# Opening of a hybrid decoder layer: x scaled row by row ahead of plain transposes, both halves of u read from PSUM, the first weight tile's pieces set between the x tiles

## The reference

```python
def rmsnorm(x, w):
    xf = x.astype(jnp.float32)
    y = xf * lax.rsqrt(jnp.mean(xf * xf, axis=-1, keepdims=True) + EPS)
    return (y * w.astype(jnp.float32)).astype(x.dtype)

    u = rmsnorm(h, norm_w)                       # h: meta tokens, then x; 1040 rows of 1024
    proj = jnp.einsum('btd,dc->btc', u, w_in)    # w_in: 1024 x 4104
    cuts = np.cumsum([HG_WIDTH, HG_WIDTH, HG_WIDTH, HG_WIDTH, 3 * GDN_WIDTH, GDN_WIDTH, GDN_HEADS])
    hg_q, hg_f, hg_i, hg_z, gd_qkv, gd_z, gd_a, gd_b = jnp.split(proj, [int(c) for c in cuts], axis=-1)
    ...
    g = -jnp.exp(gdn_A_log.astype(f32)) * jax.nn.softplus(gd_a.astype(f32) + gdn_dt_bias.astype(f32))
```

## Time and profile before

| | us |
|---|---|
| median of 3 runs | 728.11 |
| lowest, highest | 727.39, 728.21 |
| the profiled execution | 727.87 |
| its span in the trace | 726.2 |
| PE busy | 706.3 (97%) |
| DVE, ACT, POOL busy | 436.0, 304.3, 351.9 |

### The profile page before, as it was taken

How to read it: one execution, slowest core, us unless ns; L and a number is a source line. 1 busy time by engine, 2 the same in 40 slices (tenths; PEclk the granted TensorE clock), 3 DMA queues, 4 the chain that set the end, 5 groups by cost and what they waited for, 6 DMA issues and landing times. The chain is left out here.

```text
span 726.2 us, 13528 instructions
## 1 busy us (share of the span) xinstructions
PE 706.3 (97%) x4858; PEld 678.3 (93%) x4858; DVE 436.0 (60%) x1018; ACT 304.3 (42%) x800; POOL 351.9 (48%) x471
## 2 busy tenths in 40 slices
PE   7999999999999999999999999999999999999995
PEld 7799999999999999999999999999999998888884
DVE  6845356279882472598934634989436257776257
ACT  6644431635544315445444154445442352232333
POOL 5782332257562422376714232767342557756333
PEclk9999999999999999999999999999999999999999
DMA  8355332221213317450639141202244306221004
GB/s 265 35 65 84 29 34 57 50 29 31 36 33 61 53 42 64 21 39 17 40 51 71 40 69 25 35 9 48 51 67 152 86 32 209 68 64 52 30 36 195
DMA packets 63989, 44.93 MB, mean 62 GB/s; under 512 B 17438, under 2 KB 59044, under 8 KB 63924
## 3 DMA queue, kind: packets, MB, share of 16 engines
q1 hardware_dynamic: 63924, 44.07, 33.7%
HBM read 35.82 MB, written 7.65 MB: 60 GB/s over the span
## 5 line engine op out<-in xcount | busy, mean ns | idle before, releaser
L258 PE MATMUL proj<-uTh,w_high 128*128 128x352 f32 (+4 forms) x768 | 261.6, 341 | 2.4 <-PEq L1742 2.4
L258 PE MATMUL proj<-uTh,w_low 128*128 128x352 f32 (+4 forms) x768 | 246.0, 320 | 0.0
L258 PE MATMUL proj<-uTl,w_high 128*128 128x352 f32 (+4 forms) x768 | 245.5, 320 | 0.0
L258 PEld LDWEIGHTS proj<-uTh,w_high 128*128 128x128 f32 x768 | 145.3, 189 | 3.3 <-issue 3.1
L258 PEld LDWEIGHTS proj<-uTl,w_high 128*128 128x128 f32 x768 | 145.3, 189 | 0.0
L258 PEld LDWEIGHTS proj<-uTh,w_low 128*128 128x128 f32 x768 | 144.4, 188 | 0.0
L276 POOL TENSOR_TENSOR w_low<-w_raw,w_high 128x256 fp32r<-128x256 f32 (+1 forms) x54 | 71.7, 1328 | 84.0 <-ACT w_high L268 36.6
L1242 POOL TENSOR_TENSOR f_suffix<-f_suffix,f_prefix 128x192 f32<-128x192 f32 x84 | 55.5, 661 | 27.7 <-DVE f_prefix L1458 21.2
L1662 PEld LDWEIGHTS mix<-level_x 128*128 128x128 f32 x448 | 60.7, 191 | 3.4 <-issue 1.2
L1662 PE MATMUL mix<-level_x 128*128 128x64 f32 x448 | 59.8, 266 | 0.0
L1505 DVE SCALAR_TENSOR_TENSOR conv_out<-conv_in,hg_taps,conv_out 128x352 f32<-128x352 f32 (+2 forms) x81 | 51.7, 638 | 0.5
(11 more groups left out here) (308 smaller groups left out, 1397.0 us busy)
## 6 DMA issues: line engine op xcount, KB each, us to landing
w_raw<-in_w_in SPq DMA_DIRECT2D x32, 512.0 KB, 8.3
x_tile<-in_x SPq DMA_DIRECT2D x8, 512.0 KB, 6.7
w_raw<-y_scratch SPq DMA_DIRECT2D x8, 384.0 KB, 4.4
decay<-gamma_scratch SPq DMA_DIRECT2D x4, 576.0 KB, 3.7
landing<-in_w_out SPq DMA_DIRECT2D x4, 512.0 KB, 8.0
landing<-in_x SPq DMA_DIRECT2D x3, 512.0 KB, 6.4
out_y<-landing SPq DMA_DIRECT2D x3, 512.0 KB, 2.6
y_scratch<-gd_y SPq DMA_DIRECT2D x6, 192.0 KB, 1.8
```

Of the source, the lines that this page charges most:

```text
L258: last = pe.matmul(acc[:, 0:tw], w[j % 2][:, k, :], u[:, k, t0:t0 + tw], start=(k == 0 and i == 0), stop=(k == KT - 1 and i == 2))
```

## The change

- The norm weight is loaded as one row spread over 128 partitions (`nrow`, 512 KB in SBUF), between the first and the second x tile. It is no longer among the small parameter rows.
- DVE multiplies x in place by the inverse root and that row (`scale_tile`, 128x1024) before PE turns it.
- PE turns the scaled tile with plain transposes against the identity. The diagonal matrices, their ring and the copy of the identity in PSUM are gone.
- ACT rounds straight from PSUM, DVE subtracts straight from PSUM and frees the bank. POOL has no part in the low halves any more, and `u_part` is gone.
- ACT squares three tiles ahead instead of four.
- The first weight tile is loaded after x tile 5, ahead of the gate columns and of x tiles 6 to 8. ACT casts it after tile 2's halves, POOL makes its low part, in four quarters, after the inverse root of tile 5.
- On PE, parts 0 to 7 of the first piece and the first gate piece stand between the transposes of tiles 4 to 8. After tile 8 come the second piece, two gate pieces and the third piece; the gate rows are turned after the third piece and the cumulative gate is made after the fifth.
- The transpose of the parameter rows stands after tile 3. The clearing of the masks on DVE stands after the x tiles.

```diff
+            sp.dma_start(nrow[:, :], norm_w[0:1, :].broadcast_to([P, D])).then_inc(nrow_in, 16)
+            load_x(2)
+            load_x(3)
             sp.wait_ge(cleared, 1)
...
-            for i in range(2, XS):
-                load_x(i)
+            load_x(4)
+            load_x(5)
+            load_tile(0, tile_cols("gd", GD_KINDS[0], 0))
             sp.dma_start(gate_raw[:, :, :], w_in_v[:, :, AB_COLS:AB_COLS + 2 * HEADS]).then_inc(gate_in, 16)
+            load_x(6)
+            load_x(7)
...
+            for i in range(NC):
                 rstd_tile(i)
-            for i in range(NC):
-                low_part(pool, 2 * i + 1)
-                if i + AHEAD < NC:
-                    rstd_tile(i + AHEAD)
-            early_low(0)
+                if i == 5:
+                    pool.wait_ge(w_high, 1)
+                    for part in range(LOW_PARTS):
+                        ks = slice(part * KT // LOW_PARTS, (part + 1) * KT // LOW_PARTS)
+                        last = pool.tensor_tensor(wl[0][:, ks, :], raw[1][:, ks, :], wh[0][:, ks, :].bitcast(F32), ALU.subtract)
+                    last.then_inc(w_low, 1)
...
+            def scale_tile(i):
...
+                dve.scalar_tensor_tensor(out=x_, in0=x_, scalar=rstd[0:w, i:i + 1], in1=nrow[0:w, :],
+                                         op0=ALU.mult, op1=ALU.mult).then_inc(scaled, 1)
+
+            def low_part(i, half):
+
+                dve.wait_ge(u_high, 2 * i + half + 1)
+                dve.tensor_tensor(u_of(ul, i, half), turned(i, half), u_of(uh, i, half).bitcast(F32), ALU.subtract
+                                  ).then_inc(bank_free(front, ("x", i, half)), 1)
...
+                        last = pe.transpose(ap[:, k * P:k * P + w], xt[i % XS][0:w, c0:c0 + P], ident[0:w, 0:w])
                     last.then_inc(done, 1)
-            for g in range(len(PIECES)):
+                if i == EARLY - 1:
+                    pe.wait_ge(rows_in, 64)
+                    ap, done = take(pe, front, "rows")
+                    pe.transpose(ap[:, 0:P], rows[:, :], ident[:, :]).then_inc(done, 1)
+                if i in (EARLY, EARLY + 1):
+                    project(range(3 * (i - EARLY), 3 * (i - EARLY) + 3))
+                if i == EARLY + 2:
+                    project(range(6, PARTS))
+                    gate_piece(0, range(2))
+                if i == EARLY + 3:
+                    gate_piece(0, range(2, KT))
+            project(range(PARTS, 2 * PARTS))
+            for g in range(1, len(PIECES)):
                 gate_piece(g)
-            project(range(0, PARTS))
+            project(range(2 * PARTS, 3 * PARTS))
             pe.wait_ge(gate_out, len(PIECES))
```

More of the change, by code:

```diff
@@ L343, in hybrid_layer @@
     XS = 8
-    DIAGS = 3
     xt = [sb(f"x_tile{i}", [P, D], F32, s1) for i in range(XS)]
-    ut = [sb(f"u_part{i}", [P, 512], F32, s1) for i in range(3)]
-    diag = [sb(f"rstd_diag{i}", [P, P], F32, s1) for i in range(DIAGS)]
+    nrow = sb("norm_row", [P, D], F32, s1)
     square = sb("square", [P, D], F32, s1)
@@ L365, in hybrid_layer @@
     pmask = sb("pad_mask", [P, 1], F32, s1)
-    front = Bank(["rows"] + [("x", i, half) for i in range(NC) for half in range(2)]
-                 + [("ab", g) for g in range(NG)] + ["gam", "tot", "gam_rows"], 4)
+    EARLY = 4
+    front = Bank([("x", i, half) for i in range(EARLY) for half in range(2)] + ["rows"]
+                 + [("x", i, half) for i in range(EARLY, NC) for half in range(2)] + [("ab", g) for g in range(NG)] + ["gam", "tot", "gam_rows"], 4)
     gbank = bank[4:6]
-    ident_ps = bank[5][:, 384:384 + P]
-    AHEAD = 4
+    AHEAD = 3
     with nc.Block() as block:
@@ L519, in _, with high_part @@
         def _(act):
-            def high_part(n):
-                i, half = divmod(n, 2)
-                w = rows_of(i)
-                t0 = 0 if i == 0 else META + (i - 1) * P
-                freed(act, front, ("x", i, half))
-                act.copy(uh[:, 4 * half:4 * half + 4, t0:t0 + w],
-                         ut[n % 3][:, 0:4 * w].rearrange("p (k t) -> p k t", k=4)).then_inc(u_high, 1)
+            def high_part(i, half):
+                full(act, front, ("x", i, half))
+                act.copy(u_of(uh, i, half), turned(i, half)).then_inc(u_high, 1)
             def square_tile(i):
@@ L562, in _ @@
             for i in range(NC):
[L563 to L566 removed]
                 for half in range(2):
[L568 removed]
+                    high_part(i, half)
                 if i + AHEAD < NC:
                     square_tile(i + AHEAD)
+                if i == 2:
+                    early_high(0)
                 if i == 4:
@@ L661, in _ @@
             dve.memset(ab_t[:, 0:PAD], 0.0)
+            dve.wait_ge(nrow_in, 16)
+            scale_tile(0)
+            for i in range(NC):
+                if i + 1 < NC:
+                    scale_tile(i + 1)
+                for half in range(2):
+                    low_part(i, half)
+                if i == EARLY:
+                    lower_bounds()
+                if i == 5:
+                    dve.wait_ge(gate_high, 1)
+                    dve.tensor_tensor(gate_l, gate_raw[:, :, :], gate_h.bitcast(F32), ALU.subtract).then_inc(gate_low, 1)
             dve.memset(mwork[:, :, :], 0.0).then_inc(mask_set, 1)
@@ L760, in project, with u_ready, gate_piece @@
                     if part == 0 and j == 0:
-                        for low in u_low:
-                            pe.wait_ge(low, 1 + -(-(t0 + tw - META) // P))
+                        u_ready(t0 + tw)
                     project_part(pe, n, "front", 1)
-            def gate_piece(g):
+            def u_ready(t1):
+                for half in range(2):
+                    freed(pe, front, ("x", -(-(t1 - META) // P), half))
+            def gate_piece(g, ks=range(KT)):
                 t0, tw = PIECES[g]
-                for low in u_low:
-                    pe.wait_ge(low, 1 + -(-(t0 + tw - META) // P))
-                pe.wait_ge(gate_low, 1)
-                if g >= 2:
-                    pe.wait_ge(gate_out, g - 1)
-                for k in range(KT):
+                if ks[0] == 0:
+                    u_ready(t0 + tw)
+                    pe.wait_ge(gate_low, 1)
+                    if g >= 2:
+                        pe.wait_ge(gate_out, g - 1)
+                for k in ks:
                     for n, u in enumerate((uh, ul)):
@@ L775, in gate_piece @@
                                          start=(k == 0 and n == 0), stop=(k == KT - 1 and n == 1))
-                last.then_inc(gate_done, 1)
+                if ks[-1] == KT - 1:
+                    last.then_inc(gate_done, 1)
             pe.wait_ge(const0, 4)
-            pe.transpose(ident_ps, ident[:, :], ident[:, :]).then_inc(ident_there, 1)
-            pe.wait_ge(rows_in, 80)
-            ap, done = take(pe, front, "rows")
-            pe.transpose(ap[:, 0:P], rows[:, :], ident[:, :]).then_inc(done, 1)
             for i in range(NC):
@@ L803, in _ @@
                 last.then_inc(done, 1)
-            project(range(PARTS, 3 * PARTS))
+            project(range(3 * PARTS, 5 * PARTS))
             pe.wait_ge(gate_step, 9)
```

86 lines of the change are left out of this document (26 added, 60 removed).

## The result

The changed kernel takes **730.19 us** (median of 6 runs, 729.36 to 731.03) against 728.16 for the kernel before (6 runs beside them, 727.39 to 728.70): ratio 1.0029, 95% interval 1.0016 to 1.0042. It is 2.0 us slower; the prediction was 1.3 us faster. Its profiled execution took 730.13 us, span 728.4 (before: 727.87, span 726.2).

What follows compares the result with a forecast made beforehand. PE was taken as the bound once its opening wait ends. Start 20.2, work 10.9 and slow clock 1.75 end at 32.8 against 34.1: 727.87 - 1.3 = 726.6, plus 0.24 to the median, 726.8 us; range 723.8 to 732.5.

Steps and rivals of the forecast that it cites:

- The bound: In the opening: PE bounds once it has work without gaps; each us it gets there sooner is an us off.
- The weight tile's landing: First weight tile by DMA: lands at 16.0, 4 us behind x5, with 15 and 18 as ends.
- the rival of the late tile: First weight tile needs 5.5 to 7 us in the queue, lands at 17.4 to 18.9; at 18.9, 729.7 us; chance 0.16.
- my own sign of being wrong: Wrong if matmuls 0.29 apart behind tile 7, weight tile landing after 17.5, or PE idle before gate or decay work.
- POOL's low part: POOL on the first weight tile: 2.9 us, between 2.40 whole and 3.2 in quarters, done at 20.1.
- PE's work: From the first piece at 20.2 to tile 8's last transpose: 10.9 us, plus 1.75 for a slow clock.
- The sum of the opening: Tile 8's transposes end at 32.8, against 34.1 at the same remaining work before: 1.3 us gained.
- The clock rival: Clock stays at 1.2 GHz until tile 8 is turned: loss 7.7 us, 735.8, with partial relief 733; chance 0.12.
- Do the others keep up: ACT, DVE and x8 in the opening: never late for PE, with 1.5 to 2 us to spare.
- Later waits: Behind tile 8: nothing lost; rival that gate or decay chain waits: up to 1.3 us, 728.1, chance 0.10.
- the gate chain: Behind tile 8: 6.2 us, covered by two pieces of 7.8 us: costs nothing, 1.6 us from costing.
- the decay rows: Near the block's end: up to 2 us late, DVE idles 3.47 us before its last convolution: costs nothing.

Runs made afterwards that it cites:

- the low part whole: Changed kernel with POOL's low part of the first weight tile in one 128x1024 instruction instead of four quarters: 727.58 us, ratio 0.9990.
- the wide fillers: Kernel with the low part whole plus 48 transposes of 16x16 ahead of x tile 0 and 24 of 128x128 between tile 4's halves: 727.13 us, ratio 0.9982.
- the first half of the change: Changed kernel with weight tile, gate columns and their products put back behind x tile 8; scale and plain transposes stay: 729.84 us, ratio 1.0019.
- the old number of PE instructions: 72 unread 16x16 transposes added on PE: to the changed kernel 729.30 us, ratio 1.0019; to the kernel with the low part whole 728.03 us, ratio 1.0000.
- the kernel with the later cast: Changed kernel with ACT's cast of the first weight tile one x tile later, behind tile 3's halves and square 6: 732.55 us, ratio 1.0054.
- The shifted kernel: Kernel before plus 56 transposes of 16x16 that nobody reads: 729.07 us, ratio 1.0016.

## Why the prediction was wrong, point by point

- **The bound** was right: from the first product on PE never stands in this stretch, and a us of its start is a us of the opening's end, as the profile with the low part whole shows (1.4 for 1.4).
- **The weight tile's landing is the step that failed.** I put it at 16.0, 4 us behind x5, and it came at 18.6: x5 landed at 12.4 instead of 11.9, and the weight tile 6.2 us behind it. Both ends of my 3 to 6 us were worked out, not read. The trace of the kernel before has x8 at 17.7, not 16.2, so its first weight tile landed 1.8 behind the tile ahead, and the second 5.0 behind the first. Neither shows what such a tile costs among x tiles; the 7.9 us that it pushes x2 back is the number that was missing. This is the rival of the late tile, to which I gave 0.16, and my own sign of being wrong (a landing after 17.5). That its numbers (18.9, 729.7 us) come so near is in part luck: it had all of its loss, 1.6, in the opening, where the first profile lost 0.9.
- **POOL's low part** was mis-sized: 2.9 between 2.40 and 3.2, measured 3.77; 1.0 of it is the last quarter's meeting with DVE's scale, which the sum did not ask about. Both terms together moved the start from 20.2 to 23.65, 3.45 us.
- **PE's work** from there was too high: 35.02 - 23.65 = 11.4 instead of 12.65. At full clock the same work takes 9.9 (21.66 to 31.6 with the wide fillers) where I had 10.9; the clock then cost 1.4 in the first profile, and 2.2 in the second, where tile 8 is turned at 35.9 instead of 35.0; I had 1.75.
- **The sum of the opening**: 32.8 + 3.45 - 1.3 = 35.0. A gain of 1.3 became a loss of 0.9, in the other two profiles of 1.7 and 1.8.
- **The clock rival** did not come: the clock was up from 26.8 (28.5) on. By the Trainium skill, TensorE: Matmul & The Clock Gate, Part 4, whose numbers there are for bf16, transposes should not have counted. The trace disagrees for these fp32 ones: PE had run nothing but transposes when the granted clock rose at 13.1 in the changed kernel, where tile 2's eight take 1.75 us and tile 3's eight 1.09, and again at 20.1 with the wide fillers. It does not follow that they always raise it: in the two repeats of the changed kernel the same transposes of tiles 1 to 3 take 1.97 us for each eight, and the clock rose only at 28.5 and 28.6.
- **Do the others keep up**: yes. DVE and x8 were not late for PE. What the first half of the change costs when nothing covers it, 0.7, I had not asked: DVE's 2.39 us a tile up to 26.7, then tile 8 at the lower clock.
- **Later waits** I put at nothing, by the gate chain and the decay rows. These indeed cost nothing: the gate products start at 56.17 without a pause of PE. But I looked only for waits of the stages that the change touches. What waited was at 126 and 359 us, in stages that the change leaves alone: 1.5 us in the profile, a term that the sum did not have. With the old number of PE instructions it is gone from the profiles; for the 0.5 at 126 the instruction packet is shown as the cause, for the rest the cause stays open.

## What to carry to other kernels

Price a transfer that is moved into a busy stream by what it does to the tile behind it, not by its bytes: here 512 KB in 512-byte rows cost it 7.9 us where 512 KB in 4 KB rows cost 1.4. Put what stands alone between a landing and the first use into one instruction, and ask what the engines beside it do in that time. Give PE something of full width to do in front of the work that counts. And where a change takes away instructions of the bounding engine, compare the whole trace with the one before, not only the edited stage: its instruction transfers move, and can meet a wait that had nothing to do with the change.

## What the runs showed of the hardware

- Packets of 512 bytes went at 342 to 432 in the first us and 276 to 371 in the next, and then at 24 to 134 a us from 13 to 17 us, in every trace with the weight tile behind x5; in the changed kernel each took three to five times as long as at first. The landing differs with it: 17.6 to 19.6 us for the same place in the queue.
- One 16 KB instruction packet (0.9 to 1.5 us) beside a 72 KB read made the read land in 2.6 to 4.2 us (11 reads) instead of 2.2 to 2.4 (57 reads). It landed 2.0 to 2.4 us behind the packet's start where the packet started behind the issue.
- POOL takes 2.36 us for 128x1024. Four of 128x256 take 2.78 in the kernel with the later cast, where no scale of DVE falls into them, and 3.77 in the changed kernel, where a 128x1024 scale starts in between: the quarter behind its start takes 1.72 instead of 0.73. DVE's subtractions from PSUM, which ran beside the first quarters, did not hold them up.
- The clock's rise differs by 1.8 us between executions of one kernel. Before its first change in a trace the granted clock reads 1.00 although the products stand 0.29 apart: there only the durations tell.
- Most of the variants spread more than the kernel before: a standard deviation of 1.1 us over 12 runs with the low part whole, 1.0 with the wide fillers, and 0.6 and 0.4 for the kernel before beside them. The shifted kernel, whose opening waits for no weight tile, has 0.9 against 0.3, so the weight tile is not the whole reason. One profile is then a poor stand-in for the median, by 0.5 to 1.8 us here.
